# Turning sixteen-bit planes of the attention probabilities back into words: on GpSimd in place of ScalarE

## The chip, the cores and the metric

The kernel runs on one core of one Trainium2 chip. The metric is device time in microseconds, as the median of several runs of the whole program. Five engines work side by side: TensorE (PE), VectorE (DVE), ScalarE (ACT), GpSimd (POOL) and SyncE (SP, which only issues transfers). Each takes its own instructions in the order in which they are written, and semaphores join them.

## The reference

One layer over 256 tokens of width 2048: an RMS norm, one input projection of width 9296, two attentions of 8 heads of 128 each, gates, one output projection, the residual and a last RMS norm.

```
h = rms_norm(x, norm_gain)
qa, ka, va, ga, qb, kb, vb, gb, qi, ki, wi = split(h @ w_in)
A: scores = qa.ka * 128**-0.5 + rel_bias, masked by chunks of 64, softmax, times va
B: indexer sum_h w[t,h] relu(qi[t,h].ki[s]) picks 64 keys a query;
   scores = qb.kb * 128**-0.5 - slope * distance on these, softmax, times vb
y = concat(A * silu(ga), B * silu(gb));  out = rms_norm(x + y @ w_out, final_gain)
```

Everything is float32.

## The kernel before

All large products are made in split form: a float32 number is written as a high part, which ScalarE makes by a copy into a reduced format, and a low part, which VectorE makes by subtracting (`split_hi`, line 759; `split_lo`, line 1080). A product is three matmuls, high x high, high x low and low x high (`mm3`, lines 513 to 518).

**Blocks and units.** The weights come in blocks of 512 columns; a block `g` has 8 units of 512 KB, and a unit is twelve matmuls. A ring of 4 slots holds units. SP loads unit c of a block once VectorE has made the low part of the unit three places ahead of it (`lo_done`), since that frees a slot's landing place. Chunks are numbered on through the next block: split (g, 10) is unit 2 of block g + 1.

**Pairs of heads.** Eight blocks (g = 10 to 17) each carry one pair of heads beside their projection. In block g = pair + 10, PE makes the scores after unit 1 (`score_pair`); VectorE adds bias or distance, takes maxima and normalises (`probabilities`); ScalarE does the exponentials. Then the probabilities must be transposed. A transposing DMA handles 16-bit elements only, so `planes_out` (line 954, ScalarE) separates the low and high halves of the words into two planes, SP issues the transposing DMA `turn_planes` (line 387), right after the load of unit 2 of the next block, and `pT_out` (lines 956 to 961, ScalarE) puts the halves back together into `probs_T` and then makes the high part `pT_hi`. VectorE makes the low part (`pT_rest`, line 1432), and PE multiplies with the values (`value_pair`, from line 698), after unit 0 of the next block, or after unit 2 of the output block G_OUT for the last pair.

**Projections.** The block's own result is transposed in the same manner, by number n = pair + 4: ScalarE copies it out of PSUM into `z` (`projection_out`, line 874), GpSimd separates the halves (`split_projection`, line 491), SP issues the transpose after the load of unit 6 (`turn_projection`, line 413), and GpSimd puts the words together (`join_late`, line 497). For the last four (n = 8 to 11) this gives the gates: ScalarE takes a pair's output out of PSUM (`output`, line 966) after it has waited for the join, then a tanh; VectorE multiplies (`gated`, lines 1440 and 1443).

**The output blocks.** From G_OUT = 18 on PE multiplies y with w_out. Unit u of G_OUT needs the high and low parts of y, `y_hi(u)` (line 1006) and `y_lo(u)` (line 1471). The last gate, of n = 11, is what units 6 and 7 are made from.

**Order around the change.** It is all written out by hand. ScalarE, in a block: exps, split 6, planes_out, split 7, output, splits 8 and 9, stage_q, pT_out, split 10, projection_out, splits 11 to 13; in the last one projection_out comes ahead of pT_out. VectorE's last block runs splits 6 and 7, gating of n = 10, split 8, y_lo 0 and 1, split 9, y_lo 2 and 3, split 10, pT_rest, the split of unit 3, y_lo 4 and 5, the splits of units 4 and 5, the gating of n = 11, the split of unit 6 and y_lo(6). GpSimd in these blocks only separates and joins projections and issues two loads of x.

`probs_T` holds the indexer's keys earlier in the kernel, and `planes_T` lies in the same memory as the indexer's queries.

Of the kernel before, what the change touches and what calls it, by code (L numbers as in the profile page):

```python
# [20 lines left out]
HEADS = 8  # L21
# [37 lines left out]
def hybrid_block(nc, xT, x, norm_gain, w_blocks, w_narrow, rel_bias, wo_blocks, final_gain, out):  # L59
# [4 lines left out]
    ACT = mybir.ActivationFunctionType  # L64
# [3 lines left out]
    with ExitStack() as ctx:  # L68
        def sb(name, shape, dt=f32):
            return ctx.enter_context(nc.sbuf_tensor(name, shape, dt))  # L70
# [4 lines left out]
        def sem(name):  # L75
            return ctx.enter_context(nc.semaphore(name))
# [26 lines left out]
        probs_T = sb("probs_T", [P, 2, P + T])  # L103
# [83 lines left out]
        keys_made = sem("keys_made")  # L187
# [40 lines left out]
        planes_turned = sem("planes_turned")  # L228
        words_made = sem("words_made")
# [28 lines left out]
        N_LATE, N_GATE, N_END = 4, 8, 12  # L258
# [3 lines left out]
        def flat(t):  # L262
            return t.rearrange("p a b -> p (a b)")
# [31 lines left out]
        planes_T = flat(qiT[:, :, :]).bitcast(u16)[:, 2 * WORDS:4 * WORDS].rearrange("p (s n) -> p s n", s=2)  # L295

        def halves(words):
            return flat(words[:, :, :]).bitcast(u16).rearrange("p (n s) -> p s n", s=2)
# [3 lines left out]
        def proj_planes(n):  # L302

            if n < N_GATE:
                at = D * (n >= N_LATE)
                pair = (o_flat[:, at:at + PROJ_WORDS], o_flat[:, at + PROJ_WORDS:at + 2 * PROJ_WORDS])
            else:
                pair = (v1_flat[:, 0:PROJ_WORDS], flat(t_gate[:, :, :]))
            return [t.bitcast(u16).rearrange("p (s n) -> p s n", s=2) for t in pair]

        def proj_home(n):

            if n >= N_GATE:
                return halves(z).rearrange("p s (c n) -> p s c n", c=2)
            first, step = ((0, 2), (4, 2), (1, 2), (5, 2), (0, 1), (2, 1), (4, 1), (6, 1))[n]
            return qk[:, :, :].bitcast(u16).rearrange("p c (n s) -> p s c n", s=2)[:, :, first:first + step + 1:step, :]
# [5 lines left out]
        def narrow_loads(p):  # L322

            return sum(kind == BROAD and q % RING == p % RING for q, (kind, _) in enumerate(STARTS[:p + 1]))
# [122 lines left out]
        @block.gpsimd  # L447
        def _(pool):
            pool.dma_start(gain[:, :], norm_gain).then_inc(gain_landed, 16)
            nc.gpsimd.memset(ones[:, :], 1.0).then_inc(cleared, 1)  # L450
            for h in range(HEADS):
                nc.gpsimd.memset(neg_slope[:, h:h + 1], -(2.0 ** (-8.0 * (h + 1) / HEADS))).then_inc(cleared, 1)
            nc.gpsimd.iota(dist[:, :], pattern=[[-1, T]], base=P, channel_multiplier=1,
                           allow_small_or_imprecise_dtypes=True).then_inc(patterned, 1)
            pool.wait_ge(xT_landed[UNITS - 1], 16)
            pool.dma_start(bias_ext[:, 0:2 * MAX_REL + 1], rel_bias).then_inc(row_landed, 16)

            pool.wait_ge(ext_ready, 1)
            pool.dma_start(ext_dram, bias_ext[:, :]).then_inc(ext_stored, 16)

            def split_q(i):

                pool.wait_ge(feat_out, i + 1)
                for h in range(2):
                    nc.gpsimd.tensor_tensor(qi_twice[h][rows[h], :], qiT[rows[h], i, :],
                                            ones[rows[h], :].broadcast_to((IDX_D, 2 * QT)),
                                            ALU.mult).then_inc(qhi_done, 1)
                for h in range(2):
                    pool.wait_ge(qhi_done, 2 * i + h + 1)
                    pool.dma_start(qi_twice[h][rows[1 - h], :], qi_twice[h][rows[h], :]).then_inc(qi_doubled, 16)  # L470
                for h in range(2):
                    nc.gpsimd.tensor_tensor(qi_lo[rows[h], :], qiT[rows[h], i, :],
                                            qi_twice[h][rows[h], :].bitcast(f32), ALU.subtract).then_inc(qnow_ready, 1)

            split_q(0)
            pool.wait_ge(ext_stored, 16)
            pool.wait_ge(summed, UNITS)
            windows = bass.AP(tensor=ext_dram.tensor, offset=ext_dram.offset + 1,
                              ap=[[1, P], [3 * P, HEADS], [1, T]])
            pool.dma_start(bias_back, windows).then_inc(bias_landed, 16)  # L480
            for i in range(1, 4):
                pool.wait_ge(iscored0, i)
                split_q(i)

            pool.dma_start(fgain[:, :], final_gain.partition_broadcast(P)).then_inc(fgain_landed, 16)

            def split_projection(n):
                pool.wait_ge(proj_out, n + 1)  # L490
                nc.gpsimd.tensor_copy(proj_planes(n)[0], halves(z)).then_inc(proj_split, 1)  # L491
                pool.wait_ge(proj_split, n + 1)

            pool.wait_ge(qnow_ready, 8)
            def join_late(n):
                pool.wait_ge(proj_turned, 16 * n + 16)
                nc.gpsimd.tensor_copy(proj_home(n), proj_planes(n)[1].rearrange("p s (c n) -> p s c n", c=2)  # L497
                                      ).then_inc(proj_joined, 1)
                pool.wait_ge(proj_joined, n + 1)

            x_rows = x_flat.rearrange("p (m d) -> p m d", m=TM)
            for n in range(N_LATE, N_END):
                split_projection(n)
                join_late(n)
                if n == N_END - 2:
                    pool.wait_ge(scored, HEADS)
                    pool.dma_start(x_rows[:, :, 0:CB], x[:, :, 0:CB]).then_inc(res_landed, 16)
            pool.dma_start(x_rows[:, :, CB:D], x[:, :, CB:D]).then_inc(rest_landed, 16)
# [242 lines left out]
        def _(act):  # L751
# [202 lines left out]
                nc.scalar.activation(planes, halves(probs), ACT.Copy).then_inc(planes_made, 1)  # L954

            def pT_out(pair):
                act.wait_ge(planes_turned, 16 * pair + 16)
                nc.scalar.activation(halves(probs_T), planes_T, ACT.Copy).then_inc(words_made, 1)  # L958
                act.wait_ge(words_made, pair + 1)
                nc.scalar.activation(pT_hi.rearrange("p (h t) -> p h t", h=2), pT0,  # L960
                                     ACT.Copy).then_inc(pt_hi_done, 1)
# [11 lines left out]
            def pair_attention(g, pair, staged):  # L973
                exps(pair, pair < 4)
                split_hi(g, 6)
                planes_out(pair)
                split_hi(g, 7)
                if pair > 0:
                    turned_back(pair - 1)
                if pair > 4:  # L980
                    tanh_gates(pair - 5)
                split_hi(g, 8)
                split_hi(g, 9)
                stage_q(*staged)
                pT_out(pair)
                split_hi(g, 10)
                if pair > 4:
                    act.wait_ge(y_done, 2 * (pair - 4))
                projection_out(g)
                split_hi(g, 11)  # L990
                split_hi(g, 12)
                split_hi(g, 13)
# [31 lines left out]
            act.wait_ge(y_done, 6)  # L1024
            projection_out(g)
            pT_out(HEADS - 1)
            split_hi(G_OUT, 3)
            y_hi(4)
# [552 lines left out]
```

## Time and profile before

| | |
|---|---|
| median of 3 runs | 516.11 us (516.06 to 516.22) |
| the profiled execution's own time | 516.02 us |
| its span | 514.2 us |
| busy PE, VectorE, ScalarE, GpSimd | 505.7, 354.3, 305.7, 70.1 us |
| ScalarE's copies of line 958 | 8, 15.6 us in all |

A row of the timeline says when an instruction started, how long it took, and in brackets how long its engine had been idle and who ended that. The span leaves out what lies around the program's instructions, so the execution's own time is 1.8 us more.

### The profile page before, as it was taken

What the parts mean: (1) busy time and instruction counts of PE and PEld (TensorE: products, weight loads), DVE (VectorE), ACT (ScalarE), POOL (GpSimd) and SP (SyncE); (2) the same over time, 40 slices, a digit from 0 to 9 for tenths busy, and PEclk for the clock granted to TensorE, in tenths of its full rate; (3) what the DMA queues carried; (4) which work ended last, traced back from release to release, by engine and by line L of the source; (5) the groups of instructions that cost most, each with busy time, mean ns of one, the idle gap of its engine ahead of it and who ended that gap; (6) DMA issues with size and microseconds to landing.
All of it is one profiled execution on the core that took longest, in us unless ns stands there. A gap on an engine that the chain in (4) does not pass through costs nothing.

```text
span 514.2 us, 6764 instructions
## 1 busy us (share of the span) xinstructions
PE 505.7 (98%) x2476; PEld 430.1 (84%) x2476; DVE 354.3 (69%) x517; ACT 305.7 (59%) x410; POOL 70.1 (14%) x61
## 2 busy tenths in 40 slices
PE   8999999999999999999999999999999999999994
PEld 6989999888888888888888888888888888888883
DVE  5897777765856686876777766666768687746554
ACT  6866555446564555445866758584959586545342
POOL 1000053150500000000111130303021313000000
PEclk9999999999999999999999999999999999999998
DMA  8974898658685876563768676877677779775614
GB/s 270 401 234 142 215 296 265 241 184 237 236 256 164 246 208 224 201 193 102 246 198 240 212 245 215 214 216 205 194 206 229 233 222 267 266 223 178 202 41 164
DMA packets 77358, 112.23 MB, mean 218 GB/s; under 512 B 44144, under 2 KB 53264, under 8 KB 77200
## 3 DMA queue, kind: packets, MB, share of 16 engines
q1 hardware_dynamic: 75472, 106.38, 67.4%
q0 software_dynamic: 1568, 5.01, 3.0%
q10 hardware_dynamic: 288, 0.46, 0.3%
q8 instruction: 17, 0.28, 0.2%
q14 instruction: 13, 0.11, 0.1%
HBM read 99.24 MB, written 2.11 MB: 197 GB/s over the span
## 4 chain that ended last, share of the span: by engine, by line
PE 98%; DMA 1%; DVE 0%; ACT 0%; issue 0%; DVEq 0%; POOLq 0%
PE acc L516 26%; PE acc L518 25%; PE acc L517 25%; PE acc L547 5%; PE acc L567 4%; PE acc L575 3%; PE acc L551 2%; PE aux L577 2%; DMA gain<-norm_gain 1%; PE aux L688 1%; PE aux L698 1%; PE aux L686 0%; PE aux L703 0%; PE aux L704 0%; PE aux L685 0%; PE aux L705 0%
## 5 line engine op out<-in xcount | busy, mean ns | idle before, releaser
L1080 DVE TENSOR_TENSOR lo_slots<-raw_slots,hi_slots 128x1024 fp32r<-128x1024 f32 x166 | 210.4, 1278 | 108.7 <-ACT hi_slots L759 108.1
L759 ACT ACTIVATE hi_slots<-raw_slots 128x1024 fp32r<-128x1024 f32 x166 | 174.0, 1056 | 127.4 <-PE acc L518 110.0
L516 PE MATMUL acc<-hi_slots,acts 128*128 128x512 f32 x576 | 225.4, 391 | 0.0
L518 PE MATMUL acc<-hi_slots,acts 128*128 128x512 f32 x576 | 224.2, 389 | 0.0
L517 PE MATMUL acc<-lo_slots,acts 128*128 128x512 f32 x576 | 224.2, 389 | 0.0
L518 PEld LDWEIGHTS acc<-hi_slots,acts 128*128 128x128 f32 x576 | 108.1, 188 | 22.8
L516 PEld LDWEIGHTS acc<-hi_slots,acts 128*128 128x128 f32 x576 | 108.2, 188 | 22.1 <-DVE acts L1471 0.3
L517 PEld LDWEIGHTS acc<-lo_slots,acts 128*128 128x128 f32 x576 | 108.2, 188 | 21.8
L547 PE MATMUL acc<-acts,hi_slots 128*128 128x384 f32 x128 | 34.3, 349 | 0.0
L491 POOL COPY o<-z 128x2048 uint16<-128x2048 uint16 x4 | 7.6, 1899 | 159.7 <-ACT z L874 159.7
L551 PEld LDWEIGHTS acc<-acts,lo_slots 128*128 128x128 f32 x128 | 23.1, 188 | 0.0
L551 PE MATMUL acc<-acts,lo_slots 128*128 128x192 f32 x128 | 23.1, 262 | 0.0
L547 PEld LDWEIGHTS acc<-acts,hi_slots 128*128 128x128 f32 x128 | 19.4, 191 | 0.0
L944 ACT ACTIVATE probs<-probs,neg_top,q_rate 128x256 f32<-128x256 f32 (+1 forms) x16 | 8.6, 536 | 17.4 <-DVE neg_top L1392 17.4
L567 PE MATMUL acc<-hi_slots,acts 128*128 128x512 f32 x64 | 17.9, 394 | 0.3 <-DVE acts L1109 0.3
L575 PE MATMUL acc<-hi_slots,acts 128*128 128x320 f32 x64 | 18.0, 308 | 0.0
L577 PE MATMUL aux<-hi_slots,acts 128*128 128x272 f32 x64 | 17.6, 286 | 0.0
L958 ACT ACTIVATE probs_T<-qiT 128x1536 uint16<-128x1536 uint16 x8 | 15.6, 1947 | 2.3 <-DMA qiT<-qiT 2.3
L491 POOL COPY v<-z 128x2048 uint16<-128x2048 uint16 x4 | 8.0, 2010 | 53.7 <-ACT z L874 53.7
L497 POOL COPY z<-t_gate 128x2048 uint16<-128x2048 uint16 x4 | 12.1, 3024 | 21.4 <-DMA t_gate<-v 21.4
L567 PEld LDWEIGHTS acc<-hi_slots,acts 128*128 128x128 f32 x64 | 11.5, 188 | 3.9 <-DVE acts L1109 1.7
L947 ACT ACTIVATE probs<-probs,neg_max 128x256 f32<-128x256 f32 (+1 forms) x16 | 7.1, 446 | 11.8 <-DVE neg_max L1388 11.8
(172 smaller groups left out, 481.5 us busy)
## 6 DMA issues: line engine op xcount, KB each, us to landing
raw_slots<-w_blocks SPq DMA_DIRECT2D x140, 512.0 KB, 4.3
raw_slots<-wo_blocks SPq DMA_DIRECT2D x32, 512.0 KB, 4.2
raw_slots<-w_blocks SPq DMA_DIRECT2D x8, 256.0 KB, 5.2
qk<-xT SPq DMA_DIRECT2D x7, 256.0 KB, 5.3
qk<-x POOLq DMA_DIRECT2D x1, 1536.0 KB, 8.1
o<-ext_dram POOLq DMA_DIRECT2D x1, 1024.0 KB, 7.3
fgain<-final_gain POOLq DMA_DIRECT2D x1, 1024.0 KB, 4.8
out<-o SPq DMA_DIRECT2D x2, 512.0 KB, 3.0
```

The lines of the kernel that those rows point to most:

```text
L491: nc.gpsimd.tensor_copy(proj_planes(n)[0], halves(z)).then_inc(proj_split, 1)
L516: nc.tensor.matmul(dst, a_hi[:, k, t], hi, start=start, stop=False)
L517: nc.tensor.matmul(dst, a_hi[:, k, t], lo, start=False, stop=False)
L518: return nc.tensor.matmul(dst, a_lo[:, k, t], hi, start=False, stop=stop)
L547: nc.tensor.matmul(whole, w_hi4[:, u % RING, q, f * HD:f * HD + HD], acts[:, k, :, tokens], start=(k == 0), stop=False)
L551: last = nc.tensor.matmul(acc[:, bank:bank + n], w_lo4[:, u % RING, q, f * HD:f * HD + HD], a_hi[:, k, tokens], start=False, stop=(k == KT ...
L567: last = nc.tensor.matmul(acc[:, m * CB:m * CB + CB], a[:, k, m * P:m * P + P], w[:, p % RING, c], start=start, stop=stop)
L575: nc.tensor.matmul(acc[:, (TM + m) * CB:(TM + m) * CB + PART], a[:, k, t], w[:, p % RING, c:c + PART], start=start, stop=stop)
L577: last = nc.tensor.matmul(aux[m][:, 0:REST], a[:, k, t], w[:, p % RING, c + PART:c + WIDE], start=start, stop=stop)
L759: nc.scalar.activation(hi_slots[:, s, 0:UK * CB], w_raw[:, s, :], ACT.Copy).then_inc(hi_done, 1)
L958: nc.scalar.activation(halves(probs_T), planes_T, ACT.Copy).then_inc(words_made, 1)
L1080: nc.vector.tensor_tensor(lo_slots[:, s, 0:UK * CB], w_raw[:, s, :], hi_slots[:, s, 0:UK * CB].bitcast(f32), ALU.subtract).then_inc(lo_don ...
```

## The change

The wait for the transposed planes and the copy that joins them leave ScalarE's `pT_out`, and go to GpSimd as `join_words`. ScalarE still waits for the words and makes the high part. On GpSimd the copy of pair 0 is the first instruction of the loop, that of pairs 1 to 6 comes behind the join of the projection of the pair before, and that of pair 7 behind the join of n = 10 and the first load of x, ahead of the separation of n = 11.

```
+            def join_words(pair):
+                pool.wait_ge(planes_turned, 16 * pair + 16)
+                nc.gpsimd.tensor_copy(halves(probs_T), planes_T).then_inc(words_made, 1)
+                pool.wait_ge(words_made, pair + 1)
+
             x_rows = x_flat.rearrange("p (m d) -> p m d", m=TM)
+            pool.wait_ge(keys_made, 1)
+            join_words(0)
             for n in range(N_LATE, N_END):
+                if n == N_END - 1:
+                    join_words(HEADS - 1)
                 split_projection(n)
                 join_late(n)
+                if n < N_END - 2:
+                    join_words(n - N_LATE + 1)
                 if n == N_END - 2:
                     pool.wait_ge(scored, HEADS)
                     pool.dma_start(x_rows[:, :, 0:CB], x[:, :, 0:CB]).then_inc(res_landed, 16)
...
             def pT_out(pair):
-                act.wait_ge(planes_turned, 16 * pair + 16)
-                nc.scalar.activation(halves(probs_T), planes_T, ACT.Copy).then_inc(words_made, 1)
                 act.wait_ge(words_made, pair + 1)
```

## Rows read from the trace of the kernel before

**Rows 1.** The page's first part: busy time, share of the span and instructions, by engine.
```profile
PE 505.7 (98%) x2476; PEld 430.1 (84%) x2476; DVE 354.3 (69%) x517; ACT 305.7 (59%) x410; POOL 70.1 (14%) x61
```
**Rows 2.** The waits: who waited for whom, us in total, times, the longest.
```profile
PE acc L558 <- DVE probs_T L1104: 1.1, 1, 1.1
PEld acc L516 <- DVE acts L1471: 0.3, 1, 0.3
```
**Rows 3.** The chain of waits in order of time: start us, us, what.
```profile
252.23 0.44 PE aux L698 x4
373.00 0.44 PE aux L698 x4
426.74 0.44 PE aux L698 x4
436.09 0.42 PE acc L516
```
**Rows 4.** The timeline of ScalarE, 418 to 431: start us, us, engine, line.
```profile
418.68 1.27 ACT L874 ACTIVATE z<-acc,rstd 128x512 f32<-128x512 f32 x2 [1.58 <-PE acc L518]
419.83 1.97 ACT L958 ACTIVATE probs_T<-qiT 128x1536 uint16<-128x1536 uint16 x1
...
430.55 0.60 ACT L966 ACTIVATE o<-aux 128x512 f32<-128x512 f32 x1 [4.19 <-POOL z L497]
```
**Rows 5.** The timeline of GpSimd, 408 to 431.
```profile
420.01 2.36 POOL L491 COPY v<-z 128x2048 uint16<-128x2048 uint16 x1 [13.16 <-ACT z L874]
426.98 3.53 POOL L497 COPY z<-t_gate 128x2048 uint16<-128x2048 uint16 x1 [4.61 <-DMA t_gate<-v]
```
**Rows 6.** The timeline of SP's issues, 409 to 425.
```profile
409.81 1.71 SPq L387 DMA_TRANSPOSE qiT<-qiT  x1
412.02 8.95 SPq L342 DMA_DIRECT2D raw_slots<-wo_blocks  x4
422.40 2.60 SPq L413 DMA_TRANSPOSE t_gate<-v  x1
```
**Rows 7.** The timeline of VectorE, 414 to 436.
```profile
414.73 1.22 DVE L1080 TENSOR_TENSOR lo_slots<-raw_slots,hi_slots 128x1024 fp32r<-128x1024 f32 x1
...
419.40 1.22 DVE L1080 TENSOR_TENSOR lo_slots<-raw_slots,hi_slots 128x1024 fp32r<-128x1024 f32 x1
422.50 0.69 DVE L1432 TENSOR_TENSOR parts_lo<-probs_T,parts_hi 128x512 fp32r<-128x512 f32 x1 [1.88 <-ACT parts_hi L960]
...
425.80 2.36 DVE L1080 TENSOR_TENSOR lo_slots<-raw_slots,hi_slots 128x1024 fp32r<-128x1024 f32 x2
...
435.27 0.68 DVE L1471 TENSOR_TENSOR acts<-o,acts 128x512 fp32r<-128x512 f32 x1
```
**Rows 8.** Timelines of GpSimd and VectorE at 260; then a group of the page.
```profile
259.33 2.50 POOL L497 COPY qk<-o 128x2048 uint16<-128x2048 uint16 x1 [4.40 <-DMA o<-o]
...
260.48 1.37 DVE L1392 TENSOR_SCALAR neg_top<-neg_max,q_rate 128x2 f32<-128x2 f32 x1
...
L491 POOL COPY o<-z 128x2048 uint16<-128x2048 uint16 x4 | 7.6, 1899 | 159.7 <-ACT z L874 159.7
```
**Rows 9.** Issue to landing, of the planes' transposes (line 387), then the projections' (413).
```profile
DMA to landing us min/median/max: 4.8/4.9/5.0
...
DMA to landing us min/median/max: 4.3/4.4/6.6
```
**Rows 10.** Timelines of ScalarE and VectorE in pair 0, then VectorE in pair 5.
```profile
248.36 1.94 ACT L958 ACTIVATE probs_T<-qiT 128x1536 uint16<-128x1536 uint16 x1 [1.01 <-DMA qiT<-qiT]
...
248.10 0.68 DVE L1359 TENSOR_TENSOR parts_lo<-qk,parts_hi 128x512 fp32r<-128x512 f32 x1
251.00 0.69 DVE L1432 TENSOR_TENSOR parts_lo<-probs_T,parts_hi 128x512 fp32r<-128x512 f32 x1 [2.22 <-ACT parts_hi L960]
...
369.67 0.69 DVE L1432 TENSOR_TENSOR parts_lo<-probs_T,parts_hi 128x512 fp32r<-128x512 f32 x1
```

## The prediction

> **What bounds the kernel now.** I read the busy shares first: TensorE (PE) is busy 98% of the span [rows 1], so only a change that makes PE wait, or takes one of its waits away, can move the end. Next the waits: those of PE are 1.1 us for its first operand and one of 0.3 us on a y_lo of VectorE, line 1471 [rows 2]. In the chain of waits the pieces on PE follow each other, and past the start the one that shows that 0.3 us is the matmul at 436.09 [rows 3]: unit 6 of block G_OUT, which needs y_lo(6). So nothing can be gained but about 0.3 us; the question is whose lateness reaches PE.
>
> The wait at 436 has a long tail. Its chain: ScalarE copies the last projection out (418.68 to 419.95) [rows 4]; GpSimd splits it (420.01 to 422.37); SP issues the transposing DMA at 422.40 [rows 6]; GpSimd joins from 426.98 to 430.51 [rows 5]; ScalarE's output(7) starts at 430.55, then come tanh, gating and y_lo(6), which ends at 435.27 + 0.68 = 435.95 [rows 4, 7]. From the join's end to y_lo(6) are 5.44 us that the change leaves alone. Each 0.1 us that the join ends later is 0.1 us on PE and on the end.
>
> **The change, part by part.** *Removed:* eight ScalarE copies of 1.95 to 1.97 us (1.97 for pair 7 [rows 4]), 15.6 us in all. ScalarE waits for PE or VectorE in every block, so the saving is worth nothing by itself. *Added:* eight GpSimd copies of 128x1536 16-bit elements with the same kind of strided write as the join (line 497). The undisturbed join takes 2.50 us for 2048 elements [rows 8]; by columns, 2.50 x 1536/2048 = 1.88 us. Bounds: 1.42 us (the rate of the split, 1.90 us for 2048 [rows 8]) and 2.65 us (the slow join's 3.53 us scaled [rows 5]). I take 1.88, since read and write patterns are those of the join. ScalarE's wait for the words replaces the wait for the DMA; before, the copy's end and the next instruction lay 0.04 us apart, and a join's end and output(7) also 0.04 [rows 4, 5], so the hand-over costs nothing. The moved wait for keys_made at the head of the loop is long satisfied.
>
> *What GpSimd does to VectorE.* Here the price lies. In rows 8 the join of 259.33 ends at 261.83, and a VectorE tensor_scalar on two columns that started at 260.48 took 1.37 us and ended at 261.85: it stood until GpSimd was done. The other way, the join of 426.98 took 3.53 us, not 2.50: it started while VectorE ran a pair of tensor_tensor until 428.16 [rows 5, 7]. So the two don't overlap; one stands for the other's instruction. The Trainium skill says the same, SBUF — State Buffer, section "SBUF: two separate sides": an exclusive lock on a shared port pair, held for the whole instruction, against VectorE instructions with two SBUF inputs or in a two-port mode. This trace agrees (1.37 us for a two-column instruction, 3.53 against 2.50). By a view in which the engines share nothing, the sum below would be 0.
>
> *Pairs 0 to 6.* The narrowest place is pair 0: VectorE's pt_lo (line 1432) ends at 251.00 + 0.69 = 251.69 [rows 10] and value_pair starts at 252.23 [rows 3]: cover 0.54 us. The planes are there at 248.36, VectorE's tensor_tensor of line 1359 runs to 248.78 [rows 10], GpSimd then copies until 250.66, ScalarE's old copy ended at 250.30: 0.36 of the 0.54 used. Later covers are larger: pair 5, 369.67 + 0.69 = 370.36 against 373.00 [rows 3, 10], 2.64 us. There VectorE has gating, two splits' work and stage_rest to do when the planes land, and the copy holds it up for 1.9 us; 0.7 us are left. Pair 6 repeats this. In pairs 1 to 3 the cover lies between these two, and the lateness of the join delays the maxima of the next pair (as in rows 8), an estimated 0.2 us a pair, the rest of one short instruction. I put pairs 0 to 6 at 0, with 0.5 us as the price if pair 0's cover goes and its lateness is carried on.
>
> *Pair 7.* The planes' DMA is issued at 409.81 [rows 6] and lands 4.9 us later [rows 9], at 414.7. GpSimd is idle then, so the copy is done by about 417.7 and doesn't queue ahead of the split at 420.01. But VectorE works without a gap from 414.73 to 419.40 + 1.22 = 420.62 [rows 7]: the split of unit 0 of G_OUT, y_lo(0), y_lo(1), the split of unit 1, y_lo(2), y_lo(3), and lo(10), the split of unit 2. All of these read two SBUF operands. The copy takes 1.88 us out of this run, so lo(10) would end near 422.4; and then the split of GpSimd at 420.0, which before fell into the tail of this run (2.36 us, 0.47 longer than the usual 1.90 [rows 5, 8]) and left VectorE idle 1.88 us afterwards, falls into its middle and takes another 1.90. Together 420.62 + 1.88 + 1.90 = 424.4, less about 0.2 for the overlap of starts: lo(10) at 424.2. It doesn't matter who wins a hand-over: if VectorE finishes first, lo(10) is at 422.5 and the split is done at 424.2.
>
> SP's order is load of unit 6 (waits for lo(10)), then turn_projection(11) (waits for the split). Before, that load was the last of the four, issued until 420.97, and the transpose went at 422.40 [rows 6]. Now load 6 goes at 424.2 and the transpose 0.35 us later, at 424.55: 2.15 us later. Landing after issue: 4.4 us median, 6.6 the most [rows 9], this one 426.98 - 422.40 = 4.58. The load now stands right ahead of it on the queue, as it does ahead of the planes' transposes (4.9 for less data), so I take 5.0: 429.55. VectorE by then has pt_lo, the split of unit 3, y_lo(4) and y_lo(5), and the splits of units 4 and 5 to do, 0.6 + 1.15 + 1.2 + 2.3 = 5.3 us from 424.2: done at 429.5, so the join finds the ports free and takes 2.50: it ends at 432.05. Before: 430.51. The difference, 1.5 us, is the forecast. The ends: 4.4 us to landing, join waits to 429.5 and ends 432.0 less the overlap, +1.3; 6.6 us to landing, join ends at 433.65, +3.1. PE's unit 2 needs lo(10) too. A block takes (373.00 - 252.23)/5 = 24.15 us [rows 3], a unit of its eight about 2.7 beside the pair's own matmuls, and unit 2 ends where value_pair(7) starts, at 426.74, so it starts at about 424.0: a wait of 0.3 us, which is swallowed by the larger one at unit 6.
>
> ScalarE is free 1.9 us earlier (419.95), but all it feeds there (pt_hi, y_hi(4), y_hi(5) and the high parts of units 3 to 5) then waits for VectorE.
>
> The profiled execution's own time is 516.02 against a span of 514.2, and the median of the runs is 516.11. Span 514.2 + 1.5 = 515.7, time 516.02 + 1.5 = 517.5, and with the 0.1 by which the median stands above it 517.6.
>
> **The rivals.**
> 1. *The ports cost less than the run of VectorE can take; no change.* The copy of 1.42 us, a split that slips into an early gap, and a transpose that lands within 4.4 us would leave +0.3 to +0.9 on the join, and half of it could be caught up in gating. For it: the join before stood 1.01 us waiting for VectorE (3.53 against 2.50 [rows 5, 8]), which is a reserve. Against: SP's load waits for lo(10), and no reserve lies ahead of that. Time 516.0 to 517.0, middle 516.5.
> 2. *Faster.* ScalarE's 1.97 us at 419.83 go, VectorE's idle 1.88 us ahead of pt_lo [rows 4, 7] go with them, the pair of splits at 425.80 runs 1.9 us earlier and the join at 426.98 starts at once: 2.50 rather than 3.53, and PE's 0.3 us vanish. It decides if the copy at 414.7 doesn't stand in VectorE's way. Time 516.11 - 0.3 = 515.8; no more, since PE has no other wait to lose [rows 2].
> 3. *A loop over the pairs.* Copy late, projection copied late, join late, maxima late (rows 8 shows that link at work), planes late. Each turn of pairs 0 to 3 adds its wait for VectorE; if that is the 0.7 us of a whole tensor_tensor [rows 7] rather than 0.2, then 0.36 + 3 x 0.7 = 2.5 us by pair 3 use up its cover, and PE waits 0.3 to 1 us there, and again at pairs 5 and 6. With the 1.5 of pair 7: 518.5 to 520.5, middle 519.3.
> 4. *The copy is not where it is said to be:* if the wait for proj_turned ahead of it held GpSimd past the landing, the copy would come late. GpSimd has been idle for 13.16 us when it starts at 420.01 [rows 5], since 406.85, 8 us before the planes land; this I leave out.
>
> In GPSIMD Engine Reference, section "Elementwise — side-by-side cycle accounting", the Trainium skill gives 1.03 cycles per element for the simplest bodies, an estimate of 1.3 us for 1536 at 1.2 GHz. The trace's join is slower, 2.50 us for 2048; by the page the forecast would be 0.5 us less.
>
> **How the numbers follow.** Forecast 0.60 (its own range 517.0 to 519.2), no change 0.22, faster 0.08, loop 0.10. Under 0.2% (1.03 us) a difference can't be told from none: the time counts as slower above 517.14. From the forecast 0.56 lies above it, from the loop 0.09, from rival 1 0.01: slower 0.66. Faster needs 515.08, which no case reaches; 0.02 stays for what I don't see. Same 0.32. The range of 8 in 10 goes from 515.9 (rival 1 whole, rival 2 out) to 519.3 (the middle of the loop, and the longest landing).
>
> **What the profile after would show.** Right: a GpSimd copy of some 1.9 us near 414.7, the y_lo and splits behind it 1.9 us later, one VectorE instruction near 420 stretched by almost 2 us, the last t_gate transpose issued near 424.5, the join's end near 432, and at unit 6 a wait of PE of about 1.8 us. Wrong: if the last transpose is still issued near 422.4 (then the ports don't matter), if PE waits at a value_pair of pairs 0 to 6 (the loop), or if the copies take far from 1.9 us. ScalarE busy less by 15.6 us and GpSimd more by some 15 shows only that the change is in.

## The result and the profile after

The changed kernel takes 518.9 us in the median of 6 runs (518.28 to 521.7), the kernel before, on the same chip, 516.33. The ratio is 1.006, 95% interval 1.0045 to 1.0074: 3.1 us slower, between 2.3 and 3.8 (the two medians differ by 2.6). The sign of the forecast and its mechanism for pair 7 held; its 1.5 us were about half of what came.

The profiled execution is the slowest of the six (521.7, span 519.9 against 514.2), so what it shows is more than what the median lost. Line numbers shift from kernel to kernel; the text says what stands in a line where it matters. The page's first part:
```profile
PE 507.4 (98%) x2476; PEld 429.4 (83%) x2476; DVE 368.2 (71%) x517; ACT 290.7 (56%) x402; POOL 87.7 (17%) x69
```
ScalarE is down by 15.0 us and GpSimd up by 17.6, as the moved copies make it [rows 1]. VectorE has the same 517 instructions and is "busy" 13.9 us longer: since the work is the same, that is time in which its instructions stood waiting. The waits (us in total, times, longest):
```profile
ACT parts_hi L969 <- POOL probs_T L503: 17.6, 7, 3.3
...
PE acc L527 <- DVE acts L1480: 1.4, 1, 1.4
...
PE acc L527 <- DVE lo_slots L1089: 1.0, 1, 1.0
...
PE aux L709 <- DVE parts_lo L1441: 0.8, 1, 0.8
PE acc L578 <- ACT hi_slots L814: 0.7, 1, 0.7
```
Before, PE waited once past the start, 0.3 us [rows 2]. Now it waits at three kinds of places. Line 1480 is y_lo, as in rows 2; line 1089 is a split; line 709 is value_pair, line 1441 pt_lo. The 0.7 us are at 9 us into the span, long before the change acts, and have nothing to do with it; the wait for the first operand, 1.1 us as before, is left out. The chain of waits dates the rest (start, us, what):
```profile
326.92 0.71 PE aux L709 x4
...
399.63 0.45 PE aux L709 x4
...
441.67 0.50 PE acc L527
```
Against rows 3, where value_pair(5) starts at 373.00 and so, blocks of 24.15 us apart, value_pair(3) at 324.70 and value_pair(6) at 397.15: PE is 2.2 us late at pair 3, 2.5 at pair 6, and 441.67 - 436.09 = 5.6 at unit 6 of G_OUT. Of this 0.9 us is older than the change: the subtraction that rows 10 have at 248.10, ahead of the first moved copy, starts at 249.00 here. So the copies of pairs 0 to 3 account for 1.3 us.

The tail of pair 7, on GpSimd and on SP:
```profile
419.73 2.42 POOL L503 COPY probs_T<-qiT 128x1536 uint16<-128x1536 uint16 x1 [7.43 <-DMA qiT<-qiT]
422.56 2.98 POOL L491 COPY v<-z 128x2048 uint16<-128x2048 uint16 x1 [0.41 <-ACT z L885]
433.68 2.51 POOL L497 COPY z<-t_gate 128x2048 uint16<-128x2048 uint16 x1 [8.14 <-DMA t_gate<-v]
```
```profile
428.21 3.36 SPq L413 DMA_TRANSPOSE t_gate<-v  x1
```
The separation ends at 422.56 + 2.98 = 425.54, but the transpose goes at 428.21, 2.7 us later. Before, it went 0.03 us after the separation [rows 5, 6]. That is the step of the forecast: the transpose stands behind the load of unit 6, and the load waits for a split that the two GpSimd copies held up. (A load waits for the split four units earlier, since the ring has four slots: unit 6 for unit 2, not "three places ahead".)

The two other places are new. At pair 6, GpSimd, then VectorE, then SP, then GpSimd and VectorE again:
```profile
398.40 1.90 POOL L491 COPY v<-z 128x2048 uint16<-128x2048 uint16 x1 [3.03 <-ACT z L885]
...
398.45 5.19 DVE L1089 TENSOR_TENSOR lo_slots<-raw_slots,hi_slots 128x1024 fp32r<-128x1024 f32 x3
...
401.77 3.34 SPq L413 DMA_TRANSPOSE t_gate<-v  x1
...
408.75 2.53 POOL L497 COPY z<-t_gate 128x2048 uint16<-128x2048 uint16 x1 [8.45 <-DMA t_gate<-v]
...
409.75 2.33 DVE L1435 TENSOR_SCALAR probs<-probs,p_inv 128x256 f32<-128x256 f32 x4
```
GpSimd's separation of n = 10 starts 0.05 us before VectorE's split of unit 2 and keeps the ports for 1.9 us. Before, the two lay 1.25 us apart, the split ahead (394.77 and 396.02). The load waits for that split, the transpose for the load: it goes 1.5 us after the separation. It also lands late, the join starting 7.0 us after the issue where it was 4.4 before (397.94 to 402.32); why, no run here settles. So the join starts 6.4 us later than before, falls on VectorE's normalising (2.33 us for what takes 1.01) and puts off the planes of pair 7. And at pair 2, VectorE's stage_rest (line 1368), then GpSimd:
```profile
297.58 0.69 DVE L1368 TENSOR_TENSOR parts_lo<-qk,parts_hi 128x512 fp32r<-128x512 f32 x1
...
297.63 2.43 POOL L503 COPY probs_T<-qiT 128x1536 uint16<-128x1536 uint16 x1 [10.14 <-DMA qiT<-qiT]
```
Here VectorE is ahead, by 0.05 us, and GpSimd waits for 0.5 of its 0.69 us: 2.43 us instead of 1.92.

### The profile page after: what moved, and what is told of

Its sections match the earlier page's. It is cut to its first block, busy times and chain, and to the rows that moved or that the text cites. A ratio compares the mean times of both kernels' runs of the same rounds, so it can differ in the third digit from the quotient of the medians.

```text
span 519.9 us, 6772 instructions
## 1 busy us (share of the span) xinstructions
PE 507.4 (98%) x2476; PEld 429.4 (83%) x2476; DVE 368.2 (71%) x517; ACT 290.7 (56%) x402; POOL 87.7 (17%) x69
## 4 chain that ended last, share of the span: by engine, by line
PE 30%; DVE 9%; ACT 5%; DMA 5%; POOL 2%; issue 2%; DVEq 0%; SPq 0%; ACTq 0%; POOLq 0%
PE acc L527 10%; PE acc L529 9%; PE acc L528 9%; DMA qiT<-qiT 4%; DVE lo_slots L1089 3%; POOL probs_T L503 2%; ACT probs L955 2%; ACT hi_slots L770 1%; DVE acts L1480 1%; DVE neg_top L1401 1%; ACT qiT L965 1%; DVE probs L1412 1%; DMA t_gate<-v 1%; DVE probs L1435 1%; POOL z L497 0%
## 5 line engine op out<-in xcount | busy, mean ns | idle before, releaser
L503 POOL COPY probs_T<-qiT 128x1536 uint16<-128x1536 uint16 x8 | 18.3, 2290 | 172.8 <-DMA qiT<-qiT 172.8
L588 PE MATMUL aux<-hi_slots,acts 128*128 128x272 f32 x64 | 17.6, 286 | 0.0
L969 ACT ACTIVATE parts_hi<-probs_T 128x512 fp32r<-128x512 f32 x8 | 5.1, 633 | 17.6 <-POOL probs_T L503 17.6
L497 POOL COPY z<-t_gate 128x2048 uint16<-128x2048 uint16 x4 | 10.1, 2524 | 28.2 <-DMA t_gate<-v 28.2
L965 ACT ACTIVATE qiT<-probs 128x1536 uint16<-128x1536 uint16 x8 | 11.9, 1486 | 4.1 <-DVE probs L1435 4.1
L465 POOL TENSOR_TENSOR parts_hi<-qiT,ones 64x384 fp32r<-64x384 f32 x4 | 3.6, 911 | 60.3 <-PE aux L648 44.6
```

The source lines that it names most:

```text
L503: nc.gpsimd.tensor_copy(halves(probs_T), planes_T).then_inc(words_made, 1)
L588: last = nc.tensor.matmul(aux[m][:, 0:REST], a[:, k, t], w[:, p % RING, c + PART:c + WIDE], start=start, stop=stop)
```

## The experiments

Each was run beside the kernel before; differences are ratios times 516.3 us, with the 95% interval of the ratio (0.0010 is 0.5 us). The names: "tail" is what pair 7 costs, "loop" what pairs 0 to 3 cost.

### Pair 7 alone back on ScalarE, and pair 7 alone on GpSimd

```
 def join_words(pair):
+    if pair not in ON_POOL:      # (0, ..., 6) in one kernel, (7,) in the other
+        return
...
 def pT_out(pair):
+    if pair not in ON_POOL:
+        act.wait_ge(planes_turned, 16 * pair + 16)
+        nc.scalar.activation(halves(probs_T), planes_T, ACT.Copy).then_inc(words_made, 1)
```

> The changed kernel with pair 7 alone given back to ScalarE (pairs 0 to 6 stay on GpSimd). Theory 1 (the tail of pair 7 is what costs, through VectorE's run ahead of unit 2 and SP's late transpose): 0 to 0.5 us above the kernel before, and the last t_gate transpose goes within 0.5 us of the time at which ScalarE's projection_out and GpSimd's split allow it. Theory 2 (a loop over pairs 0 to 3, each copy waiting for VectorE's stage_rest and each join holding up the next maxima): PE waits at the value_pairs of pairs 1 to 3 stay, 0.8 to 1.5 us in all, and so does that much of the time.

Measured: ratio 1.0015 (1.0001 to 1.0028), 0.8 us (0.1 to 1.4), the runs from 516.2 to 519.3. PE's wait at value_pair is there in the profile, the wait first, then the chain:
```profile
PE aux L712 <- DVE parts_lo L1447: 0.7, 1, 0.7
...
325.93 0.71 PE aux L712 x4
```
That is value_pair(3), 1.2 us later than before (324.69), 0.2 of it from ahead of the first copy. The loop is there; as a time it is at the low end of what was expected, widely spread, and barely clear of nothing. This kernel's 0.8 us also hold whatever pairs 4 to 6 cost.

> The kernel before with pair 7 alone moved to GpSimd. Theory 1 (the tail alone): 1.5 to 2.6 us above the kernel before, all of it as one wait of PE ahead of unit 6 of the first output block. Theory 2 (the loop): within 0.3 us of before. If both costs are real and add, this one and the run with pairs 0 to 6 on GpSimd sum to the 2.6 to 3.1 us of the whole change.

Measured: ratio 1.0027 (1.0013 to 1.0040), 1.4 us, just under the 1.5 to 2.6 expected, the runs within 517.8 to 518.4. Waits, then GpSimd and SP:
```profile
PE acc L530 <- DVE acts L1486: 1.3, 1, 1.3
...
416.14 2.37 POOL L506 COPY probs_T<-qiT 128x1536 uint16<-128x1536 uint16 x1 [9.12 <-DMA qiT<-qiT]
420.23 2.25 POOL L492 COPY v<-z 128x2048 uint16<-128x2048 uint16 x1 [1.72 <-ACT z L888]
429.95 2.51 POOL L498 COPY z<-t_gate 128x2048 uint16<-128x2048 uint16 x1 [7.47 <-DMA t_gate<-v]
```
```profile
424.57 3.28 SPq L414 DMA_TRANSPOSE t_gate<-v  x1
```
This is the forecast's own sum, alone on the chip: the transpose at 424.57 (forecast 424.55), the join's end at 432.46 (432.05), the time 1.4 us up (1.5). It took 5.4 us to the join where I had 5.0. By the two profiles the join's end and the span are both 2.0 us later (432.46 against 430.51, 516.2 against 514.2), inside the ratio's interval (0.7 to 2.1). The two kernels' differences add to 2.2 us, a little below the interval of the whole (2.3 to 3.8) and inside that of its repetition further down (2.0 to 3.4). Each has an interval 1.4 us wide, so these times don't show whether something arises only where both are there.

### The same copies into a spare tensor, and a memset in their place

ScalarE makes the words as before. GpSimd does the same work at the same places for nobody; the planes' next transpose also waits for it.
```
+nc.gpsimd.tensor_copy(halves(spare), planes_T).then_inc(spare_made, 1)   # first kernel
+nc.gpsimd.memset(halves(spare), 0).then_inc(spare_made, 1)               # second kernel
```

> The kernel before (ScalarE still makes the words), with the same eight GpSimd copies at the same places and under the same waits, but into a spare tensor that nobody reads. If the cost comes from GpSimd's copies standing in VectorE's way, the tail of pair 7 is all there: 1.3 to 2.0 us above before; the pairs 0 to 3 add little, since ScalarE's copy doesn't wait for VectorE. If it comes from ScalarE waiting for a slower engine, there is no difference from before (0.3 us at most).

Measured: ratio 1.0035 (1.0021 to 1.0048), 1.8 us. VectorE and GpSimd at pair 7:
```profile
417.65 2.98 DVE L1486 TENSOR_TENSOR acts<-o,acts 128x512 fp32r<-128x512 f32 x2
...
417.87 2.28 POOL L507 COPY spare<-qiT 128x1536 uint16<-128x1536 uint16 x1 [9.22 <-DMA qiT<-qiT]
```
Two y_lo that take 1.28 us without a neighbour take 2.98 beside the copy. Nobody waits for the words here, so these 1.8 us aren't there because a slower engine makes them. The 0.8 to 1.3 us up to the whole change's 2.6 to 3.1 are not covered by that: the intervals overlap, and in the changed kernel the words come late as well.

> As the run with the copies into a spare tensor, but each is a memset over the same places of the spare tensor: the same writes, no reads. If any GpSimd instruction keeps VectorE's tensor_tensor out, the time is 1.3 us or more above before, and tensor_tensor instructions that fall on a memset are stretched. If only one that reads the on-chip memory does, tensor_tensor keeps its 1.22 us beside a memset, and the time is within 0.3 us of before.

Measured: ratio 0.9997 (0.9988 to 1.0006). GpSimd, then VectorE:
```profile
415.51 1.88 POOL L507 MEMSET spare<- 128x1536 uint16 x1 [8.93 <-DMA qiT<-qiT]
...
414.45 1.22 DVE L1095 TENSOR_TENSOR lo_slots<-raw_slots,hi_slots 128x1024 fp32r<-128x1024 f32 x1
415.59 1.28 DVE L1486 TENSOR_TENSOR acts<-o,acts 128x512 fp32r<-128x512 f32 x2
```
The memset is as long as the copy (1.88 us), writes the same places, and the two y_lo beside it take 1.28. So it is GpSimd's reading that shuts out an instruction of VectorE with two operands. The Trainium skill, SBUF — State Buffer, section "SBUF: two separate sides", states this exception: two SBUF inputs matter only against a GpSimd instruction that reads SBUF. The runs agree (2.98 us beside the copy, 1.28 beside the memset).

### SP's order at pair 7

```
 for u in range(UNITS):
+    if u == 6:
+        turn_projection(N_END - 1)
     out_unit(G_OUT, u)
     if u == 2:
         turn_planes(HEADS - 1)
-    if u == 6:
-        turn_projection(N_END - 1)
```
On the kernel with pair 7 alone on GpSimd:

> The kernel with pair 7 alone on GpSimd, and SP's last turn_projection moved ahead of the load of unit 6. If the 1.4 us of that kernel come through SP (the load waits for the split of unit 2, which the two GpSimd copies hold up, and the transpose stands behind it), the transpose goes as soon as GpSimd's split is done, near 422.5 instead of 424.57, and the time falls by 1.0 to 1.4 us, to within 0.4 us of before. If the cost is the port alone, whatever SP's order, it stays at 1.2 to 1.6 us above before.

Measured: ratio 1.0000 (0.9991 to 1.0009): the 1.4 us are gone. SP's transpose:
```profile
422.75 1.84 SPq L414 DMA_TRANSPOSE t_gate<-v  x1
```
The copies still hold up VectorE as much (the two pairs of y_lo take 2.97 and 2.98 us); they cost nothing once the transpose no longer stands behind VectorE on SP. The join ends at 429.70, 0.8 us sooner than before, and PE's wait at unit 6 is gone. The tail is shown: port, then split, then load, then transpose.

On the whole change:

> The changed kernel with SP's last turn_projection moved ahead of the load of unit 6, as it was done for pair 7 alone. If the whole cost is the tail (1.5) plus the loop over pairs 0 to 3 (0.8 or more), the tail's share goes and the loop's stays: 0.6 to 1.5 us above the kernel before, with PE's waits at the value_pairs still in the trace. If the order on SP were all of it, within 0.3 us of before.

Measured: ratio 1.0017 (1.0004 to 1.0030), 0.9 us, the runs from 516.3 to 519.6. The time fits the expectation, the waits don't: PE's weight loads wait 0.2 us in all at value_pairs, and in their place PE waits 1.0 us on a split. The transpose of n = 10 went as in the profile of the change, 1.5 us after the separation, and the join started at 406.50, against 402.32 before.

### VectorE idle while the words are joined

```
-stage_rest(*staged, pair + 1)
 pT_rest(pair)
+stage_rest(*staged, pair + 1)
```

> The changed kernel with VectorE's pT_rest moved ahead of stage_rest in pairs 0 to 6, so that VectorE stands idle while GpSimd joins the words. If the loop over the pairs is fed by the copy's wait for the tensor_tensor of stage_rest (0.6 us each), the copies take 1.8 to 1.9 us instead of 2.4 in pairs 0 to 3, PE's waits at the value_pairs go (0.3 to 2 us), and what is left is the tail: 1.4 to 1.9 us above before, with a smaller spread of the runs. If not, 2.6 to 3.1 us above before as the changed kernel.

Measured: ratio 1.0045 (1.0031 to 1.0059), 2.3 us, the runs 517.7, 517.8, 518.8, 518.8, 518.8. GpSimd at pairs 1 and 3:
```profile
272.32 1.92 POOL L503 COPY probs_T<-qiT 128x1536 uint16<-128x1536 uint16 x1 [9.97 <-DMA qiT<-qiT]
...
320.81 1.92 POOL L503 COPY probs_T<-qiT 128x1536 uint16<-128x1536 uint16 x1 [10.07 <-DMA qiT<-qiT]
```
The copies take 1.92 us and in this profile, of one of the two quickest runs, PE waits at no value_pair. So the copies get their 0.5 us as stated. The time is 0.4 to 0.9 us above what I expected and isn't told apart from the changed kernel's (1.0060, and 1.0051 when repeated): what the loop costs isn't shown by this edit, and something else was left.

### Both, and the split of unit 6 early

> The changed kernel with both: turn_projection ahead of the load of unit 6, and VectorE's pT_rest ahead of stage_rest. If loop and tail are the only two costs, nothing is left: within 0.4 us of the kernel before, no PE wait at a value_pair. If there is a third cost (the copies at pairs 4 to 6, say), 0.6 us or more stay.

Measured: ratio 1.0014 (1.0005 to 1.0023), 0.7 us, the runs from 516.3 to 518.2. Something of 0.3 to 1.2 us stays, and VectorE's new order took nothing measurable off the 1.0017 of SP's alone.

```
 # ScalarE                        # VectorE
+split_hi(G_OUT, 6)              +split_lo(G_OUT, 6)
 turned_back(HEADS - 1)           gated(3, 0)
 tanh_gates(3)                    gated(3, 1)
-split_hi(G_OUT, 6)              -split_lo(G_OUT, 6)
```
Alone, on the kernel before:

> The kernel before with the split of unit 6 of the first output block (high and low part) moved ahead of the gate of the last projection, into the idle time of ScalarE (4.2 us) and VectorE (2.4 us) there. If the chain join, gate, y_lo(6) sets PE's last wait, then 1.14 us of VectorE leave this chain and PE's wait of 0.3 us goes: 0.3 us faster, no more, since no other wait is there to lose. If another chain sets it, no change.

Measured: ratio 0.9994 (0.9985 to 1.0003), 0.3 us less, which the interval doesn't part from nothing. PE's wait on y_lo is gone from the profile.

On the changed kernel:

> The changed kernel with the same move of the split of unit 6. If the wait at unit 6 is the end of the same chain as before, only longer, the move takes the whole 1.14 us of that split out of it: 1.0 to 1.2 us less than the changed kernel, so 1.4 to 2.1 us above the kernel before. If the time sits in the value_pairs of pairs 0 to 3, it changes by 0.3 us or less.

Measured: ratio 1.0033 (1.0018 to 1.0047), 1.7 us: 1.4 less than the changed kernel's 1.006, with intervals that touch, and 0.9 less than its repetition. PE's wait on y_lo(6) is 0.6 us in the profile, where the change has 1.4. It agrees with the wait at unit 6 being the end of the old chain. Its profile shows the other side of the race of pair 2 (GpSimd, VectorE):
```profile
296.84 1.92 POOL L503 COPY probs_T<-qiT 128x1536 uint16<-128x1536 uint16 x1 [10.06 <-DMA qiT<-qiT]
...
296.88 2.36 DVE L1368 TENSOR_TENSOR parts_lo<-qk,parts_hi 128x512 fp32r<-128x512 f32 x1
```
GpSimd comes 0.04 us first and its copy takes 1.92. VectorE's instruction then takes 2.36 instead of 0.69; PE has no wait at pair 3.

With all three edits:

> The same, and the split of unit 6 moved ahead of the last gate. If PE's last wait there is gone too, 0.3 us less than the kernel before (ratio about 0.9994), since PE then waits for nothing but its start; the words on GpSimd bring nothing of their own. If the GpSimd copies still cost somewhere, it is at or above the kernel before.

Measured: ratio 1.0020 (1.0009 to 1.0031), 1.0 us, the runs from 516.1 to 519.1. I had expected 0.3 us less than before; it missed.

### The changed kernel again

> The changed kernel as it is, once more, for the spread of its runs and a second profile. If the loop hangs on whether GpSimd's copy or VectorE's tensor_tensor comes first by some hundredths of a microsecond, PE's waits at the value_pairs of pairs 1 to 3 differ from the first profile while the tail's stays: 2.0 to 3.5 us above before, runs spread over 1 us or more. If the loop is fixed, the waits at pairs 1 to 3 repeat within 0.2 us.

Measured: ratio 1.0051 (1.0038 to 1.0065), 2.6 us, the runs from 518.1 to 519.8. In this profile (span 516.9) PE's weight loads wait 0.6 us in all at value_pairs, against 2.1 in the first, and at pair 6 the race goes the other way. GpSimd, then SP:
```profile
396.61 2.94 POOL L491 COPY v<-z 128x2048 uint16<-128x2048 uint16 x1 [3.11 <-ACT z L885]
```
```profile
399.57 2.01 SPq L413 DMA_TRANSPOSE t_gate<-v  x1
...
425.08 3.44 SPq L413 DMA_TRANSPOSE t_gate<-v  x1
```
VectorE's split is first (the separation takes 2.94 us), so the load isn't held up, the transpose goes 0.02 us after the separation, against 1.5 in the first profile, and the join starts 4.4 us after that (403.97), against 7.0. In the tail the transpose again goes after the load, 2.1 us behind the separation (2.7 in the first).

### SP's order in every block with a pair

After this the open question was the 0.7 us and the spread. The same swap on SP was made for n = 4 to 10 too:
```
 for u in range(UNITS):
+    if u == 6 and pair is not None:
+        turn_projection(n)
     sp.wait_ge(lo_done, g * UNITS + (u - RING + 1))
     load(u, ...)
```

> The changed kernel with turn_projection ahead of the load of unit 6 in every block that transposes a pair's planes (n = 4 to 11), not in the last alone. If the rest of the cost is the same order on SP at pairs 5 and 6, what stays is the loop over pairs 0 to 3 alone, 0 to 0.6 us above before, and in the profile each transpose of these projections goes within 0.2 us of GpSimd's separation. If not, as with the last transpose alone ahead: 0.7 to 0.9 us above before with runs up to 2 us above the lowest.

> That, and VectorE's pT_rest ahead of stage_rest in pairs 0 to 6. If SP's order and the loop are all there is, the time is within 0.2 us of before and the runs spread over less than 1.2 us. If a cost of another kind stays, 0.5 us or more above before.

> That, and the split of unit 6 of the first output block ahead of the last gate. If PE then waits for nothing but its start, 0.1 to 0.3 us less than before. If the copies on GpSimd still cost something, it is at or above before.

Measured: ratios 1.0009 (1.0000 to 1.0018), 1.0008 (0.9999 to 1.0017) and 1.0012 (1.0002 to 1.0022), that is 0.5, 0.4 and 0.6 us above before. The first, one edit on SP, takes off 2 us or more of the 2.6 to 3.1. Its runs lie within 516.2 to 517.5, where the swap of the last transpose alone left 516.3 to 519.6; but the third of these kernels has the same swap and runs up to 518.3, and the two ratios, 1.0017 and 1.0009, have intervals that overlap. So the swap of the last transpose is most of the gain, and that the earlier blocks add to it is likely, not shown. Nor does a profile show it: in the profiles of all three VectorE's split won the race at pair 6 (separations of 2.95, 2.91 and 2.91 us), as in the second profile of the change, and what the swap does when it is lost was not caught.

Of the 0.4 to 0.6 us that stay, the profile of the first has about 0.5 between value_pair(6) and value_pair(7). PE has one gap there, at the start of unit 2 of G_OUT, right behind that unit's split. The chain, then VectorE:
```profile
424.20 0.11 issue
424.31 0.47 PE acc L529
```
```profile
422.95 1.21 DVE L1091 TENSOR_TENSOR lo_slots<-raw_slots,hi_slots 128x1024 fp32r<-128x1024 f32 x1
```
Two matmuls start 0.50 us apart there (423.81 and 424.31), where it is 0.23 elsewhere: some 0.3 us, the small wait at unit 2 that the forecast named. The kernel with pair 7 alone and SP's order swapped has the same gap and measured 1.0000, since it no longer waits at unit 6; so these last tenths can't be told from nothing.

The third kernel was expected below the kernel before and isn't. No version with the words on GpSimd beats the kernel before, nor does any other of these by more than its interval.

## Why the prediction was right and where it failed

- *PE sets the end, only its waits count.* Right. 15 us off ScalarE brought nothing in any run.
- *The copy takes 1.88 us.* Right: 1.92 undisturbed; 2.29 in the mean of the change, the rest being its waits for VectorE.
- *GpSimd and VectorE shut each other out.* Right, by the copies into a spare tensor (1.8 us with no use) against the memset (nothing).
- *Pair 7.* Right in its path and in its size: 1.4 us measured alone, the transpose at 424.57 for 424.55. That it goes through SP's load of unit 6 is shown by the swap that takes all of it away. One term was off without harm: the planes landed 6.1 us after their issue, not 4.9, so the copy ran at 416.14, not near 414.7, still inside VectorE's run. The small wait at unit 2, "swallowed", is the gap of 0.3 us shown above.
- *Pairs 0 to 6 at nothing.* This step failed, and with it the forecast's size. The whole change's ratio is 1.0060 (1.0051 when repeated) where pair 7 alone has 1.0027, so these pairs add 1.2 to 1.7 us; by themselves, with pair 7 on ScalarE, they cost 0.8. PE's wait at a value_pair, named as a sign of being wrong, came. "An estimated 0.2 us a pair, the rest of one short instruction" was an average over a race whose sides lie far apart: the copy starts 0.04 us before or 0.05 us after a VectorE instruction and gets 1.92 or 2.43 us. That is rival 3, to which I gave 0.10 and a middle of 519.3. Where it is lost from pair to pair, PE loses 1.3 us by pair 3 (first profile); where it goes the other way at a pair, little (second). How much of the 1.2 to 1.7 us is this loop and how much pair 6 stays open.
- *What neither forecast nor rival had:* the order "load of unit 6, then transpose" stands in every block. I followed it for pair 7 and had said of pairs 5 and 6 only that value_pair's cover holds. VectorE's delay there of 1.9 us, which I did name, brings its split of unit 2 within 0.05 us of GpSimd's separation, and when the separation wins, the transpose of n = 10 is 1.5 us late and lands later still, the join falls on the normalising, and the planes of pair 7 start later. In the first profile PE lost 3.1 us between value_pair(6) and unit 6, in which this and the tail are one sum. That this step costs time is argued from two profiles in which it is there and the others in which it isn't; with the swap in all blocks 0.5 us are left of the whole cost, but no profile has the swap and the lost race together.
- *The range* (515.9 to 519.3) held the median. Of the six runs two did not fit in it (519.56 and 521.7).

## What to carry to other kernels

When work moves to GpSimd, its price is not in its own time but in the instructions of VectorE that read two operands beside it: lay the copies over VectorE's run and push that run out, then ask which queue waits for an instruction in it. A load that waits for a buffer and stands ahead of an urgent transfer on one queue turns a harmless delay into a chain; swapping the two was worth more here than anything done to the copies. And where two engines reach for the same port within 0.1 us of each other, price both outcomes and carry each through the whole loop: an average of them hides the costly one.

## What the runs showed of the hardware that I had not expected

- A memset on GpSimd of 1.88 us runs beside VectorE's two-operand instructions at no cost to either; a copy of 1.92 us stops them for most of its length (two y_lo took 2.98 us for 1.28). The write side alone doesn't shut them out.
- Which of two instructions 0.04 us apart comes first changes from one execution to the next. That this widens a kernel's spread isn't shown: the runs of before span 0.7 to 2.4 us in the five sets, those of the change 3.4 us in one set of six and 1.7 in the other.
- The same transposing DMA of 128x2048 16-bit elements took from 4.3 to 6.9 us to land. Right behind a 512 KB load the join started 5.4 us (424.57 to 429.95) and 7.0 us (401.77 to 408.75) after its issue, with the load swapped away 4.4 (422.75 to 427.14). A load just ahead is not the whole of it: before the change one took 6.6 us that was issued 1.6 us after the last load (373.79).
